# The first projection of a hybrid block: twelve pairs of chunks by Strassen's method, the sums of squares on column groups of TensorE

## The reference, cut to what matters

```python
proj = jnp.einsum('bld,dp->blp', n, w_in)                 # 512 tokens, 1024 inputs
conv_in, gates, scal = jnp.split(proj, [CONV_CH, CONV_CH + GATE_CH], axis=-1)   # CONV_CH = 4608
c = jax.nn.silu(centred_dwconv(conv_in, conv_w, conv_b)).astype(F32)            # 7 taps
q, k, v, xs, Bm, Cm = jnp.split(c, [...], axis=-1)        # 1024, 1024, 1024, 1024, 256, 256
q = l2_normalize(q.reshape(Bsz, L, gh, GDN_HEAD_DIM)) * (GDN_HEAD_DIM ** -0.5)
k = l2_normalize(k.reshape(Bsz, L, gh, GDN_HEAD_DIM))     # 8 heads of 128: t * rsqrt(sum(t * t) + EPS)
```

## Time and profile before

| what | us |
|---|---|
| median of 3 runs | 3101.52 (3100.12 to 3102.68) |
| the profiled execution's own time | 3101.01 |
| its span in the profile | 3099.2 |
| TensorE busy | 2865.6 (92% of the span) |
| VectorE busy | 1279.5 (41%) |
| ScalarE busy | 593.9 (19%) |

### The profile page before, as it was taken

The page is one execution under the profiler, slowest core; times in us unless marked ns, Lnnn a source line. Parts: engine busy times, 40 slices in busy tenths (PEclk is TensorE's granted clock), DMA queues, the critical chain, the costliest instruction groups (busy, mean ns, idle before and its releaser), DMA issues. The chain is left out here.

```text
span 3099.2 us, 43532 instructions
## 1 busy us (share of the span) xinstructions
PE 2865.6 (92%) x18266; PEld 1810.5 (58%) x18266; DVE 1279.5 (41%) x2275; ACT 593.9 (19%) x1408; POOL 278.0 (9%) x228
## 2 busy tenths in 40 slices
PE   8999799998959997998999999999999899999897
PEld 4544688654433335876768888778775444444343
DVE  5666566555131126952353335489313211101014
ACT  3222333322011113234011110022330000000001
POOL 0000332241000000001400000000113100000001
PEclk9999899999969997999999999999999799999998
DMA  3420000107069963220232212122020733557917
GB/s 119 91 75 28 20 17 17 56 14 283 21 248 429 429 257 120 75 75 12 111 129 82 82 55 72 44 75 96 34 97 10 281 138 121 237 227 315 399 56 286
DMA packets 81941, 413.19 MB, mean 133 GB/s; under 512 B 10563, under 2 KB 21699, under 8 KB 66036
## 3 DMA queue, kind: packets, MB, share of 16 engines
q1 hardware_dynamic: 70476, 383.70, 31.2%
q10 hardware_dynamic: 7848, 14.61, 1.9%
q0 software_dynamic: 3456, 12.58, 1.1%
HBM read 382.12 MB, written 28.76 MB: 133 GB/s over the span
## 5 line engine op out<-in xcount | busy, mean ns | idle before, releaser
L3898 PE MATMUL pgu<-gu,xg 128*64 128x320 f32 (+1 forms) x2560 | 393.0, 462 | 8.9 <-POOLq L3826 8.9
L3898 PEld LDWEIGHTS pgu<-gu,xg 128*64 128x64 f32 x2560 | 182.2, 137 | 204.3 <-issue 130.3
L312 PE MATMUL proj<-feat,w 128*128 128x512 f32 x576 | 255.9, 598 | 2.6 <-PEq L153 2.6
L3905 PE MATMUL py<-down,hm_t 128*64 128x512 f32 x880 | 200.3, 603 | 9.7 <-POOLq L3826 9.7
L312 PEld LDWEIGHTS proj<-feat,w 128*128 128x128 f32 x576 | 107.4, 191 | 124.6 <-issue 124.6
L497 DVE SCALAR_TENSOR_TENSOR mixed<-padded,taps,mixed 128x512 f32<-128x512 f32 x216 | 162.4, 752 | 7.7
L2825 DVE SCALAR_TENSOR_TENSOR conv<-vg,cols,conv 128x528 f32<-128x528 f32 x240 | 164.3, 761 | 0.0
L3967 DVE TENSOR_TENSOR hm<-sg,pgu 128x384 f32<-128x384 f32 (+1 forms) x40 | 20.8, 521 | 315.2 <-PE pgu L3898 208.6
L3905 PEld LDWEIGHTS py<-down,hm_t 128*64 128x64 f32 x880 | 61.9, 139 | 121.0 <-issue 104.5
L3850 ACT ACT_TABLE_LOAD x19 | 24.4, 1283 | 460.0 <-PE pgu L3898 279.9
L3325 DVE TENSOR_TENSOR gb<-gb,pp 128x264 f32<-128x264 f32 x66 | 28.2, 429 | 174.2 <-PE pp L3237 174.2
(11 more groups left out here) (593 smaller groups left out, 4880.0 us busy)
## 6 DMA issues: line engine op xcount, KB each, us to landing
gu<-in_moe_gu SPq DMA_DIRECT2D x16, 3072.0 KB, 13.4
gu<-in_moe_gu SPq DMA_DIRECT2D x16, 2560.0 KB, 15.8
ring<-in_w_gate SPq DMA_DIRECT2D x16, 2048.0 KB, 13.3
ring<-in_w_up SPq DMA_DIRECT2D x16, 2048.0 KB, 14.7
ring<-in_w_down SPq DMA_DIRECT2D x16, 2048.0 KB, 17.0
w<-in_w_in SPq DMA_DIRECT2D x13, 2048.0 KB, 7.9
down<-in_moe_down SPq DMA_DIRECT2D x8, 3072.0 KB, 18.6
down<-in_moe_down SPq DMA_DIRECT2D x8, 2560.0 KB, 20.6
```

The costliest lines, as they stand in the source:

```text
L312: last = pe.matmul(proj[:, n % 2, :], w[:, g % 2, k, c * P:(c + 1) * P], core.feat[:, k, :], start=k == 0, stop=k == DK - 1)
L3898: last = pe.matmul(pgu[half(h), part, 0:n], xg[:, k, :], w[:, k, h, :], start=k == 0, stop=k == DK - 1)
L3905: last = pe.matmul(py[half(h), :], hm_t[:, c, :], down[:, c, h * BANK:(h + 1) * BANK], start=c == 0, stop=c == XC - 1)
```

## The change

The chunks 0 to 23 are made as twelve pairs. A pair is a product of 1024 x 256 weights with 1024 x 512 tokens; split in halves each way, it takes seven products of half the inputs (4 matmuls of 128x128 weights each) and 256 tokens instead of eight. Four sums of weights are made for each pair (`sum_weights`; one of them in place in the weights' buffer) and four sums of inputs once (`sum_inputs`), all on VectorE. The products gather in three half banks: each is copied out by ScalarE before the next one is added to the same bank, and VectorE adds three kept copies to make the rows whole (`add`). The first tap goes to ScalarE (Identity with scale and bias), the six others are made for both chunks of the pair by turns. The last twelve chunks stay as they were but for the first tap. The squares are summed four chunks at a time: `pick` has a column of ones at place b, and the four matmuls write to four groups of 32 partitions; the 16 lines of lengths are then copied and turned once (`turn_lengths`, inside pair 10). Several scratch tiles lie in tiles that are filled later (`core.chan` from 24 on, `tok_v`, `tok_x`, `tok_b`).

```diff
+                def multiply(bank, lhs, rhs, begin):
+                    for k in range(KH):
+                        last = pe.matmul(bank, lhs[:, k, :], rhs[:, k, :], start=begin and k == 0, stop=k == KH - 1,
...
+                    last.then_inc(product, 1)
+                def pair(r, between):
...
+                    multiply(bank_x(r), weight(r, 0, 0), x11, True)
+                    if r:
+                        pe.wait_ge(copied, PRODUCTS * (r - 1) + P3 + 1)
+                    multiply(bank_y(r), weight(r, 0, 1), x21, True)
+                    if between:
+                        between()
+                    pe.wait_ge(w_summed, 4 * r + 2)
+                    pe.wait_ge(x_summed, 2)
+                    pe.wait_ge(copied, PRODUCTS * r + P1 + 1)
+                    multiply(bank_x(r), s2(r), t2, False)
+                    pe.wait_ge(copied, PRODUCTS * r + P2 + 1)
+                    multiply(bank_z(r), s1(r), t1, True)
+                    pe.wait_ge(w_summed, 4 * r + 4)
+                    pe.wait_ge(x_summed, 4)
+                    pe.wait_ge(copied, PRODUCTS * r + P6 + 1)
+                    multiply(bank_x(r), s3(r), t3, False)
+                    pe.wait_ge(copied, PRODUCTS * r + P5 + 1)
+                    multiply(bank_z(r), s4(r), x22, False)
+                    pe.wait_ge(copied, PRODUCTS * r + P7 + 1)
+                    multiply(bank_x(r), weight(r, 1, 1), t4, False)
...
+                for r in range(PAIRS1):
+                    pair(r, turn_lengths if r == 10 else None)
...
+                    if r in (3, 5, 7, 9):
+                        measure((r - 3) // 2)
...
+                for n in range(PLAIN, CCH):
+                    chunk(n)
+                    for m in (n - 4, n - 3) if n == PLAIN else (n - 3, n - 2) if n == PLAIN + 1 else (n - 2,):
+                        turn(m)
...
+                for r in range(PAIRS1):
...
+                    copy(r, P1, kept(r, 0), bank_x(r))
...
+                    copy(r, P4, row(r, 1)[:, 0:HALF1], bank_x(r))
+                    act.wait_ge(added, ADDED * (r + 1))
+                    act.wait_ge(copied, PRODUCTS * (r + 1))
+                    first_tap(2 * r)
+                    first_tap(2 * r + 1)
+                    if r == 3:
+                        softplus()
...
+                for n in range(PLAIN, CCH):
+                    act.wait_ge(projected, n - PLAIN + 1)
...
+                    act.activation(padded(n)[:, PAD:PAD + SEQ], plain_bank(n), ACT.Copy).then_inc(filled, 1)
...
+                    first_tap(n)
+                    for m in (PLAIN - 2, PLAIN - 1) if n == PLAIN else (n - 1,):
+                        activate(m)
+                    for m in () if n == PLAIN else (n - 5, n - 4) if n == PLAIN + 1 else (n - 4, n - 3) if n == PLAIN + 2 else (n - 3,):
+                        move(m)
...
+                sum_weights(1)
+                for r in range(PAIRS1):
+                    add(r)
+                    if r == 9:
+                        key_lengths()
+                    convolve((2 * r, 2 * r + 1))
+                    if r + 2 < PAIRS1:
+                        sum_weights(r + 2)
```

More of the change, by code:

```diff
@@ L245, in project_first @@
     groups = CCH // GRP
+    KH, HALF1 = DK // 2, SEQ // 2
+    (P1, P2, P6, P5, P7, P3, P4) = range(7)
+    PRODUCTS = 7
+    ADDED = 3
+    PAIRS1 = X0 // 2
+    PLAIN = 2 * PAIRS1
+    SQUARES = 8
+    QUAD = 4
     NORMS = 2 * GH
@@ L281, in tl, with plain_bank, row @@
+        def plain_bank(n):
+            return proj[:, n % 2, :]
+        def row(r, a):
+            return padded(2 * r + a)[:, PAD:PAD + SEQ]
         def tl(t):
@@ new lines, in convolve @@
+                def convolve(chunks):
+                    for j in range(1, TAPS):
+                        for e, n in enumerate(chunks):
+                            if j == 1:
+                                dve.wait_ge(begun, n + 1)
+                            else:
+                                dve.wait_ge(tapped, chunks[0] * (TAPS - 2) + (j - 2) * len(chunks) + e + 1)
+                            dve.scalar_tensor_tensor(out=mixed(n), in0=padded(n)[:, j:j + SEQ], scalar=taps[:, n, j:j + 1], in1=mixed(n),
+                                                     op0=ALU.mult, op1=ALU.add).then_inc(convolved if j == TAPS - 1 else tapped, 1)
@@ new lines, in _ @@
+                sum_weights(0, (0, 1))
+                for n in range(2):
+                    sum_inputs(n)
+                sum_weights(0, (2, 3))
+                for n in range(2, 4):
+                    sum_inputs(n)
+                sum_weights(1)
[6 more added lines that the diff above has]
+                        sum_weights(r + 2)
+                    if r == 1:
```

260 lines of the change are left out of this document (180 added, 80 removed).

## The result

The change made the kernel slower by a quarter of a per cent: median 3109.82 us (8 runs, 3107.18 to 3114.3) against 3102.42 (8 runs, 3099.73 to 3108.35) of the kernel before beside it, ratio 1.0023 with an interval of 1.0013 to 1.0034. The forecast was 3093.0, with 3081 to 3101 as its range: the time lies 17 us above the forecast, 9 outside the range, and on the other side of no change. The profiled execution has a span of 3106.1 us, where before it was 3099.2.

A forecast was written before the change was run, and what follows sets the result against it. Only TensorE's time was taken to count until another engine makes it wait. Chunk 24 starts 19 us earlier, the stretch behind loses 11, and with the end 8.3 is gained: 3093.0 us, range 3081 to 3101.

The forecast's parts named there:

- everything behind the barrier moves along: Behind the barrier after the first block: all later work starts earlier by the same 8.3 us gained before it.
- Step (1): TensorE's products: a pair takes 12.08 us in place of 13.9, saving 20.0 us over pairs 1 to 11.
- Step (2): Pair 0 saves nothing, as VectorE's sums wait for the taps' load; pair 1 starts at 40.8 us.
- Step (3): Sums of squares on column groups: two groups at a time, 2.2 us per eight records, 3.9 us saved.
- Step (4): VectorE keeps nearly even: its loop per pair is 12.6 us against TensorE's 12.1, taps by turns 0.68 each.
- Step (5): Pair 4: TensorE waits 2.7 us for a copy behind ScalarE's rate functions; 1.9 us of lost clock charged separately.
- Step (6): Pair 11: its third product waits 2.1 us because VectorE makes the key lengths in pair 10.
- The hand-over: From pairs to plain chunks: turns wait for ScalarE's moves, 6.9 us together, plus 3.8 us of half clock.
- A: Rival for TensorE's waits of 3 us: the clock holds, 5.7 us come back, 3087 us; chance 25%.
- B: Rival for the pairs: VectorE bounds them, taps by turns at 0.78 us, loop 13.9, 3099.5 us; chance 13%.
- C: Rival for the clock: 7 us at half rate after each of five waits, 17.5 us lost, 3105 us; chance 8%.
- D: Rival for the lengths: no second group runs alongside, 3.5 us per eight records, 3097 us; chance 7%.

The follow-up runs named there:

- e1: The change with ScalarE's store of the bias lines moved from pair 4's round to plain chunk 28's: 3095.99 us, ratio 0.9974.
- e2: The change with the store of the bias lines issued in pair 6's round in place of pair 4's: 3110.63 us, ratio 1.0028.
- e9: e8 with 164 satisfied waits added at the head of TensorE's program: 3088.30 us, ratio to the kernel before 0.9951.
- e10: e8 with 86 satisfied waits added at the head of TensorE's program: 3081.46 us, ratio to the kernel before 0.9930.
- e11: e4 with 88 satisfied waits added at the head of TensorE's program: 3100.46 us, ratio to the kernel before 0.9994.
- e13: e8 with 84 satisfied waits on TensorE spread over the twelve plain rounds: 3076.63 us, ratio to the kernel before 0.9919.
- e14: e8 with 168 satisfied waits on TensorE spread over the twelve plain rounds: 3070.54 us, ratio to the kernel before 0.9892.
- e15: The change with 84 satisfied waits on TensorE spread over the twelve plain rounds: 3105.63 us, ratio to the kernel before 1.0005.
- e8: e7 with VectorE's wait for the taps' coefficients moved from ahead of pair 0's sums to ahead of its first taps: 3080.84 us.
- e4: The kernel before with only the change's sums of squares on four column groups: 3088.09 us, ratio 0.9953.
- e6: e1 with VectorE's taps of a pair made one chunk after the other, not by turns: 3101.77 us, ratio to the kernel before 1.0002.
- e5: e1 with ScalarE's moves issued one round earlier at the hand-over to plain chunks: 3090.35 us, ratio to the kernel before 0.9961.
- e7: e5 with ScalarE's softplus moved from the end of pair 3's round to behind two copies of pair 4's: 3083.50 us.

## Why the forecast was wrong

**Wrong: "only TensorE's time counts, until another engine makes it wait", with no term for the loads of weights.** The forecast priced the engines' work and the one load that the change made VectorE wait for. A ring of two weight groups was filled by loads of which group 4's had 8.6 us to spare before, beside a store that the profile of the kernel before showed as a DMA share of some 0.5 over 44 us. The change moved three things at once: it shortened the time from the load's issue to the group's use (31.7 to 28.4 us), it issued the load earlier by 10.2 us (120.9 to 110.7), and it delayed the store by 9.2 (89.9 to 99.1), so the end of the store, 148.4, moved past the time at which the group is needed, 139.1. This is about 15 us: 10.6 of waiting, 2.3 of half clock behind it, and most of a further wait of 2.06. e1 and e2 show it. With the store moved, the change lands 13.8 us lower (15.2 by the ratios), at 3096.0, inside the range. That it lands there is partly luck: in e1 the lengths gave 4.7 us more than priced, and the scan took 5.2 more than before.

**Wrong: "everything behind the barrier moves along".** It does not: the scan is 3.7 us longer. The change's instructions (18462 matmuls in place of 18266, all of the 196 ahead of it) move the borders at which TensorE waits for its instructions, and these waits add up to 12.7 us in the scan in place of 8.3. e9 to e11 and e13 to e15 show that moved borders do this. Behind the scan nothing is lost.

**Step (1), pairs at 12.08, right.** Pair 1 starts at 40.76 and pair 2 at 52.90, 12.1 us. e1, without the load's wait, starts chunk 24 at 193.35, forecast 194.4.

**Step (2), pair 0 saves nothing, right.** Pair 1 starts at 40.76, forecast 40.8, with a wait of 1.45 at the third product, forecast 1.5. e8, without the wait for the coefficients, starts pair 1 at 39.96.

**Step (3), lengths, right in kind and mis-sized.** I took two groups at a time, 2.2 us per eight records, from the row with 0.228 each. They take 1.0, all four groups at once, and the four of them with the turn 4.4 in place of 9.1: 4.7 us more gained than forecast, 8.8 by e4 in place of 3.9. The 7 which I gave as the bound was too low as well: it was 13.0 less 3.6 and 0.4 and should have read 9. The Trainium skill ("TensorE: Matmul & The Clock Gate", Part 3, Packing small matmuls), with 2.38 times the speed for three column tiles, was nearer than my row: eight records one after another would take 3.5 by the forecast's estimate, and 1.0 is 3.5 times the speed for four.

**Step (4), VectorE, right.** A round of 12.75 us, forecast 12.6; taps by turns 0.67, forecast 0.68; in sequence 0.77, forecast 0.78. e6 shows that the order is worth 5.8 us by the medians and 8.7 by the ratios. By the rule of the Trainium skill named there ("VectorE: DVE Perf Modes", Rules for kernel authors) this edit should have done nothing, and the measurement decides. One price was low: the first tap on ScalarE takes 0.81 (L516, 806 ns), not SiLU's 0.63.

**Step (5), pair 4, mechanism right, size low.** The wait is 3.29, forecast 2.7, and sixteen records behind it start the next block after 6.5 us in place of 3.45; forecast 1.9 of lost clock, measured 3.0 in this trace and 1.7 in e1.

**Step (6), pair 11, right.** 1.98, forecast 2.1.

**The hand-over, right.** Two waits of 3.17, forecast 3.15 each; the 0.6 more at one of them did not come. The clock costs 1.1 and 0.6 behind the first, 1.7 behind the second, 3.4 in all, forecast 3.8. From chunk 24 to the last product's end it is 98.1 us (208.25 to 306.37), forecast 100.0. e5 shows that the moves' order alone made it.

**The rivals.** A (the clock holds) failed: half clock stands behind four of the waits. B failed on its premise, e6 shows its price. C gave the nearest time, 3105, but not by its mechanism: it had 7 us at half rate, 3.5 lost, behind each of five waits, 17.5 in all. Measured were 3.0 at pair 4, 1.7 behind each of the two at the hand-over, and nothing at pairs 0 and 11, 6.4 in all. D failed. Chunk 24 started after 198, the forecast's own sign of B or C, and it was neither. No rival named the load or the instruction pieces; the 16.8 us between 3093.0 and 3109.8 are 15.2 of the load and the store and 3.7 of the scan, less the 4.7 that the lengths gave beyond their price, 0.9 by which the kernel before itself stood higher in this comparison (3102.4 and 3101.5), and 1.7 that is left over and not traced.

## What to carry to other kernels

When an edit makes a stretch shorter, write down for each load in it when it is issued, when it is needed, and what else is in flight; a load's median time says nothing about one that runs beside a slow transfer. Its longest landing, set against the time until it is needed, shows whether there is any slack. Change in separate steps where parts can stand alone: here the smaller part alone gave 15 us, and what the larger part gave was hidden by a store, by ScalarE's order and by instruction borders. A few microseconds gained or lost behind an edit, in code that it doesn't touch, may be only where the borders of TensorE's instruction pieces fall: look at the issue waits there, and add some harmless instructions before believing in another cause. Run a program's twin with the same instructions as well, since one trace differs from the next by some us too.

## What the hardware did that I had not expected

- A store of 2232 KB to scratch memory, each head's row written 128 times, ran at 50 GB/s on about half of the DMA engines' time, 44 to 48 us from its first packet to its last. It stretched a 2048 KB load on another queue from 7.9 us, the median, to 39.0 (38.3 in e2), and to 23.0 before.
- TensorE waits 0.2 to 2.0 us for its instructions at some of the borders that come every 126 to 128 matmuls, in dense runs of small ones. These waits add up to between 6.6 and 15.1 us of a scan of 260 to 271, and each ends 1.2 to 1.7 us after an instruction transfer of 16,384 bytes. With 84 added instructions e13 ran 4.2 us faster than e8, with nothing computed otherwise.
- At the program's head instructions that only check a satisfied wait are not free: TensorE's first matmul came 5.0 us later for 86 of them (e10) and 12.8 for 164 (e9), though its inputs were ready at the same time. In the plain rounds 168 cost nothing that the timeline shows.
- Four column groups of 32 rows with 512 columns each run side by side: eight records in 1.0 us.
- The same idle time doesn't always lower the clock: behind 2.00 us at pair 11 sixteen records took 3.69 in e1 and e5, at 2.4 GHz, and 5.38 in e7, e8 and e14, part of them at 1.2 GHz.
